# A two-layer hybrid decoder step on one core: the first layer norm split between setup and recurrence, all late modulation in the recurrence, the odd mixer's gating in the trunk

## What is computed

```python
mod = silu(c) @ ada_w[l] + ada_b[l]              # l = 0, 1; 6 * D columns
sh1, sc1, g1, sh2, sc2, g2 = split(mod, 6)
h = rms_norm(x, norm_g[l, 0]) * (1 + sc1) + sh1
m = even_mixer(h) if l == 0 else odd_mixer(h)
x = x + g1 * rms_norm(m, norm_g[l, 1])
h = rms_norm(x, norm_g[l, 2]) * (1 + sc2) + sh2
x = x + g2 * rms_norm(square(relu(h @ w1)) @ w2, norm_g[l, 3])
# inside odd_mixer
u, a, gt = split(h @ w_in)
glu = a * sigmoid(gt)
cv = depthwise_conv(concat([conv_hist, glu]), conv_w, width=31)
```

## Time and profile before

| what | us |
|---|---|
| median of 3 runs | 3334.59 |
| lowest, highest | 3334.08, 3335.05 |
| the profiled execution's own time | 3334.32 |
| span of its trace | 3332.6 |
| TensorE busy | 3019.7 (91%) |
| VectorE busy | 1193.7 (36%) |
| ScalarE busy | 971.1 (29%) |
| GpSimd busy | 540.4 (16%) |

### The profile page before, as it was taken

How to read it: one execution, slowest core, us unless ns; L and a number is a source line. 1 busy time by engine, 2 the same in 40 slices (tenths; PEclk the granted TensorE clock), 3 DMA queues, 4 the chain that set the end, 5 groups by cost and what they waited for, 6 DMA issues and landing times. The chain is left out here.

```text
span 3332.6 us, 44375 instructions
## 1 busy us (share of the span) xinstructions
PE 3019.7 (91%) x18088; PEld 2688.9 (81%) x18088; DVE 1193.7 (36%) x1924; ACT 971.1 (29%) x1418; POOL 540.4 (16%) x318
## 2 busy tenths in 40 slices
PE   5799999889877888999999998798697999999997
PEld 3689989733343788999999998793597999999997
DVE  4156552166622173222222226304345222222225
ACT  2233432257642242221111223220442211222221
POOL 1210111121112211221221211110121112211220
PEclk7899999999999889999999999899798999999998
DMA  5322222220064311211221113116221111101112
GB/s 226 114 84 83 78 83 91 91 88 1 0 185 151 117 62 50 68 59 57 69 63 56 57 57 128 44 26 145 92 87 44 32 44 50 50 29 46 50 50 96
DMA packets 240860, 250.38 MB, mean 75 GB/s; under 512 B 9203, under 2 KB 196007, under 8 KB 240453
## 3 DMA queue, kind: packets, MB, share of 16 engines
q1 hardware_dynamic: 226389, 219.53, 21.7%
q0 software_dynamic: 4320, 14.16, 1.4%
q10 hardware_dynamic: 10016, 14.80, 1.2%
HBM read 207.82 MB, written 29.99 MB: 71 GB/s over the span
## 5 line engine op out<-in xcount | busy, mean ns | idle before, releaser
L616 PE MATMUL PS<-trunk_x_hi,trunk_w_hi 128*128 128x364 f32 x2208 | 741.0, 336 | 94.9 <-POOL trunk_w_lo L763 37.5
L617 PE MATMUL PS<-trunk_x_lo,trunk_w_hi 128*128 128x364 f32 x2208 | 737.3, 334 | 0.0
L618 PE MATMUL PS<-trunk_x_hi,trunk_w_lo 128*128 128x364 f32 x2208 | 735.5, 333 | 0.0
L771 POOL TENSOR_TENSOR trunk_w_lo<-trunk_w_raw,trunk_w_hi 128x1024 fp32r<-128x1024 f32 x128 | 306.9, 2397 | 1354.6 <-ACT trunk_w_hi L979 1264.3
L616 PE MATMUL PS<-hidden,trunk_w_hi 128*128 128x364 f32 x1536 | 509.9, 332 | 0.0
L616 PEld LDWEIGHTS PS<-trunk_x_hi,trunk_w_hi 128*128 128x128 f32 x2208 | 424.2, 192 | 102.7 <-POOL trunk_w_lo L763 38.6
L617 PE MATMUL PS<-hidden,trunk_w_hi 128*128 128x364 f32 x1536 | 505.4, 329 | 0.0
L618 PE MATMUL PS<-hidden,trunk_w_lo 128*128 128x364 f32 x1536 | 505.1, 329 | 0.0
L617 PEld LDWEIGHTS PS<-trunk_x_lo,trunk_w_hi 128*128 128x128 f32 x2208 | 424.5, 192 | 0.0
L618 PEld LDWEIGHTS PS<-trunk_x_hi,trunk_w_lo 128*128 128x128 f32 x2208 | 423.7, 192 | 0.0
L1236 DVE TENSOR_TENSOR M<-M,PS 128x364 f32<-128x364 f32 x336 | 178.4, 533 | 465.2 <-PE PS L618 465.0
(11 more groups left out here) (365 smaller groups left out, 3445.4 us busy)
## 6 DMA issues: line engine op xcount, KB each, us to landing
trunk_w_raw<-mlp_w SPq DMA_DIRECT2D x128, 512.0 KB, 3.8
rec_ada_w<-ada_w SPq DMA_DIRECT2D x28, 1024.0 KB, 5.2
pages_k<-cache_sb_k SPq DMA_DIRECT2D x64, 256.0 KB, 3.0
rec_w_raw<-even_w_in SPq DMA_DIRECT2D x28, 512.0 KB, 3.8
pages_v<-cache_sb_v POOLq DMA_DIRECT2D x54, 256.0 KB, 3.4
x_scratch<-x_new ACTq DMA_DIRECT2D x9, 1456.0 KB, 5.9
trunk_ada_w<-ada_w SPq DMA_DIRECT2D x24, 512.0 KB, 3.9
x_new<-x_scratch SPq DMA_DIRECT2D x6, 1456.0 KB, 11.0
```

What stands on the lines that cost most here:

```text
L616: pe.matmul(out, hi, xh, start=first, stop=False)
L617: pe.matmul(out, hi, xl, start=False, stop=False)
L618: return pe.matmul(out, lo, xh, start=False, stop=last)
L771: pool.tensor_tensor(wl[:, u % 4, :], raw[:, u % 2, :], wh[:, u % 4, :].bitcast(F32), ALU.subtract).then_inc(s_lo, 1)
```

## The change

Six things:

1. `residual_norm` and its stage are gone. In `setup`, ScalarE squares each token tile as it lies in rows (one Square with a running sum per tile), which gives the row sums without a tree; root and reciprocal leave `core.rstd0`. ScalarE also issues the store of x's first chunk, the loads of the recurrence's first two weight tiles, and the tap rows of the odd mixer. The ring of x tiles waits for the squares as well.
2. The recurrence's program starts with nine spreading matmuls and scales, shifts and splits x in place, chunk by chunk, on VectorE and ScalarE. SyncE first stores the other two chunks. Part c of the first tile waits for chunk c of XL.
3. All 20 chunks of modulation are in the recurrence: 40 bursts, one after every second dense part, a turn after every fourth, and `coefs` takes all seven sets of coefficients. The last `mod_add` comes before the last three parts.
4. The trunk has no modulation; its loops on SyncE and ScalarE take in one more group.
5. The trunk's tail does the sigmoid (ScalarE) and the product (VectorE) of the gating.
6. The odd mixer shifts straight from `A_` (rows of 1024 columns, with zeroed margins), the first block's 16 transfers half on SyncE's and half on ScalarE's queue. Sample columns with their history go through a small tile of their own: 16 transfers on ScalarE's queue into `T4`, for which TensorE waits once, between the prompt part and the sample part of block 0. The tap columns come from setup.

The diff, cut to what the numbers speak of:

```diff
+def first_weights(nc, es, core, tag):
+    sb, sem = scope(nc, es, tag)
+    core.raw0 = sb("raw", [P, 2, KT, P])
+    core.s_raw0 = [sem(f"w_in{i}") for i in range(2)]
+def token_chunks(ap):
+    return ap.rearrange("p (k t) -> p k t", k=KT)
...
+            act.wait_ge(s_tz, 1)
+            for g in range(NTAP):
+                n = min(4, CWID - 4 * g)
+                act.dma_start(rows_tap[16 * g:16 * g + 16, 0:n * CG].rearrange("b (s c) -> b s c", c=CG),
+                              core.conv_w[0, 4 * g:4 * g + n, :].rearrange("s (b c) -> b s c", c=CG)).then_inc(s_rows, 16)
+            act.wait_ge(s_one, 1)
+            for i in range(9):
+                n = P if i < 8 else NS
+                act.wait_ge(s_xt[i % 4], 16 * (i // 4 + 1))
+                if i >= 2:
+                    act.wait_ge(s_q, i - 1)
+                act.activation(junk[0:n, i % 2, :], xt[0:n, i % 4, :], ACT.Square, accum_out=sums[0:n, i:i + 1]).then_inc(s_q, 1)
+                if i == 4:
+                    act.wait_ge(s_xev, 3)
+                    act.dma_start(token_chunks(core.x_dram)[:, :, 0:CW], X[:, :, 0:CW]).then_inc(s_st, 16)
+            w_v = core.even_w_in.rearrange("(k p) f -> p k f", p=P)
+            for i, at in enumerate((3 * HALF, 0)):
+                act.dma_start(core.raw0[:, i], w_v[:, :, at:at + P]).then_inc(core.s_raw0[i], 16)
+            act.wait_ge(s_q, 9)
+            act.wait_ge(s_rows, 16 * (11 + NTAP))
+            act.activation(sums[:, :], sums[:, :], ACT.Sqrt, scale=1.0 / D, bias=cols(core, "eps")).then_inc(s_rt, 1)
             act.wait_ge(s_c, 1)
             act.activation(core.cT[:, :, 0:SEG], PS[:, 0, 0:KT * 16].rearrange("p (k c) -> p k c", k=KT)[:, :, 0:SEG],
                            ACT.Silu).then_inc(s_silu, 1)
             ada.copies(act)
+            act.wait_ge(s_st, 16)
...
-            pe.wait_ge(s_rows, 16 * 11)
+            pe.wait_ge(s_rows, 16 * (11 + NTAP))
+            pe.transpose(PS[:, 1, 384:384 + P], rows_tap[:, :], ident)
...
+            dve.tensor_copy(core.tap_cols[:, :], PS[:, 1, 384:384 + P])
...
-def residual_norm(nc, core, tag, X, load, m, gate, scale, shift, store, final=False):
...
-            load_group(0)
-            with sp.Fori(1, G - 1) as g:
-                load_group(g, with_mod)
-            load_group(G - 1)
+            with sp.Fori(0, G) as g:
+                load_group(g)
             sp.wait_ge(s_mm, NEXT - 24)
...
-            def mod_burst(g, b):
-                pe.wait_ge(s_wa, g * 64 + 16 * (b - 3))
-                for i in range(2):
-                    k = 2 * b + i
-                    q = pe.matmul(PS[CG * (k % 4):CG * (k % 4) + SEG, 6, :], core.cT[:, k, 0:SEG], wa[:, i, :],
-                                  start=(k < 4), stop=(k >= 4), skip_group_check=True)
-                q.then_inc(s_am, 1)
...
-            with act.Fori(1, G - 1) as g:
+            with act.Fori(1, G) as g:
                 for u in range(4):
                     high_weights_of_group(g, u)
                 rest_of_group(g)
-                if with_mod:
-                    act.wait_ge(s_am, g * 4 + 1)
-                    act.activation(mod_rows[:, :], PS[:, 6, :], ACT.Copy).then_inc(s_ar, 1)
-            for u in range(4):
-                high_weights_of_group(G - 1, u)
-            rest_of_group(G - 1)
...
+                        if q == 2 and c == 0:
+                            act.wait_ge(s_nx, 12 + 8 + i + 1)
+                            act.activation(core.GT[:, i, :], core.GT[:, i, :], ACT.Sigmoid).then_inc(s_sg, 1)
...
-                    dve.wait_ge(s_at, g)
-                    dve.tensor_tensor(core.mod[:, l + 1, :].rearrange("p (f c) -> p f c", c=SEGP)[:, bass.ds(g * 4 + 4 * CH0, 4), 0:SEG],
-                                      PS[:, 7, 0:4 * SEGP].rearrange("p (f c) -> p f c", c=SEGP)[:, :, 0:SEG],
-                                      core.ada_bT[:, bass.ds(g * 4 + (48 * (l + 1) + 4 * CH0), 4)].unsqueeze(2)
-                                      .to_broadcast([P, 4, SEG]), ALU.add).then_inc(s_as, 1)
...
+            for i in range(HT):
+                dve.wait_ge(s_sg, i + 1)
+                dve.tensor_tensor(core.A_[:, i, :], core.A_[:, i, :], core.GT[:, i, :], ALU.mult)
...
-    CHUNKS = [(0, c) for c in range(4, 12)] + [(1, c) for c in range(6)]
+    CHUNKS = [(0, c) for c in range(4, 12)] + [(1, c) for c in range(12)]
...
+            for c in range(1, NC3):
+                sp.dma_start(token_chunks(core.x_dram)[:, :, c * CW:(c + 1) * CW], KV[:, :, c * CW:(c + 1) * CW])\
+                  .then_inc(s_st[c], 16)
...
-                if 0 <= n - 2 < BURSTS:
-                    modulation(n - 2)
+                for b in range(BURSTS):
+                    if max(0, (2 * b - 1) // 3) == n - 2:
+                        modulation(b)
...
+                if n == 0:
+                    pe.wait_ge(s_xl, 2 * (c + 1))
...
-                    if n % 2 == 0 and c == 0 and 2 <= n <= BURSTS:
-                        mod_turn(n // 2 - 1)
+                    d = NC3 * n + c
+                    if d % 4 == 0 and 1 <= d // 4 <= NCH:
+                        mod_turn(d // 4 - 1)
...
+            def high(c):
+                lo, hi = c * CW, c * CW + width(c)
+                for half in range(2):
+                    act.wait_ge(s_n, 2 * c + half + 1)
+                    for k in range(4 * half, 4 * half + 4):
+                        q = act.activation(core.XH[:, k, lo:hi], KV[:, k, lo:hi], ACT.Identity,
+                                           bias=core.mod[:, 0, k * SEGP:k * SEGP + 1])
+                    if half == 1 and c == NC3 - 1:
+                        act.wait_ge(s_ns, 3)
+                        q = act.activation(core.XH[:, :, SEQ:TP], KV[:, :, SEQ:TP], ACT.Copy)
+                    q.then_inc(s_xh, 1)
+            high_weights(0)
+            high(0)
+            high_weights(1)
+            high(1)
+            high(2)
             act.wait_ge(s_lb, 1)
             act.activation(lb[:, 1, :], lb[:, 0, :], ACT.Exp).then_inc(s_la, 1)
-            high_weights(0)
-            high_weights(1)
             for n in range(NT):
...
-                    if c == NC3 - 1 and n % 2 == 1 and n < BURSTS:
-                        mod_copy(n // 2)
+                    d = NC3 * n + c
+                    if d % 4 == 3 and d // 4 < NCH:
+                        mod_copy(d // 4)
...
-                for l, g, m_at, plus in ((0, 1, 2, 0.0), (0, 2, 4, 1.0), (0, 3, 5, 0.0), (1, 0, 1, 1.0)):
+                for l, g, m_at, plus in ((0, 1, 2, 0.0), (0, 2, 4, 1.0), (0, 3, 5, 0.0), (1, 0, 1, 1.0), (1, 1, 2, 0.0),
+                                         (1, 2, 4, 1.0), (1, 3, 5, 0.0)):
...
+            def normed(c):
+                lo, hi = c * CW, c * CW + width(c)
+                if c == 0:
+                    dve.wait_ge(s_bc, 1)
+                else:
+                    dve.wait_ge(s_st[c], 16)
+                if c == NC3 - 1:
+                    x = KV[:, :, SEQ:T]
+                    sh = core.mod[:, 0, :].rearrange("p (f c) -> p f c", c=SEGP)[:, 0:KT, 1:SEG]
+                    dve.tensor_tensor(x, x, norm_rows[:, SEQ:T].unsqueeze(1).to_broadcast([P, KT, NS]), ALU.mult).then_inc(s_ns, 1)
+                    dve.wait_ge(s_ns, 1)
+                    dve.tensor_tensor(segs(x), segs(x), per_seg(scale0[:, :, 1:SEG]), ALU.mult).then_inc(s_ns, 1)
+                    dve.wait_ge(s_ns, 2)
+                    dve.tensor_tensor(segs(x), segs(x), per_seg(sh), ALU.add).then_inc(s_ns, 1)
+                for k in range(KT):
+                    q = dve.scalar_tensor_tensor(out=KV[:, k, lo:hi], in0=KV[:, k, lo:hi], scalar=scale0[:, k, 0:1],
+                                                 in1=norm_rows[:, lo:hi], op0=ALU.mult, op1=ALU.mult)
+                    if k % 4 == 3:
+                        q.then_inc(s_n, 1)
...
+            def low(c, half):
+                lo, hi = c * CW, c * CW + width(c)
+                dve.wait_ge(s_xh, 2 * c + half + 1)
+                for k in range(4 * half, 4 * half + 4):
+                    q = dve.scalar_tensor_tensor(out=core.XL[:, k, lo:hi], in0=KV[:, k, lo:hi],
+                                                 scalar=core.mod[:, 0, k * SEGP:k * SEGP + 1],
+                                                 in1=core.XH[:, k, lo:hi].bitcast(F32), op0=ALU.add, op1=ALU.subtract)
...
+                q.then_inc(s_xl, 1)
+            for c in range(NC3):
+                normed(c)
+                low(c, 0)
+                low(c, 1)
             dve.memset(PS[:, 2, :], 0.0).then_inc(s_az, 1)
             dve.memset(A[:, :, :], 0.0).then_inc(s_A0, 1)
             lower_bounds()
...
-                    if n % 2 == 0 and c == 0 and 2 <= n <= BURSTS:
-                        mod_add(n // 2 - 1)
+                    d = NC3 * n + c
+                    if d % 4 == 0 and 1 <= d // 4 <= NCH:
+                        mod_add(d // 4 - 1)
...
-            mod_add(NCH - 1)
             coefs()
...
```

(78 more changed lines are left out.)

376 lines of the change are left out of this document (58 added, 318 removed).

## The result

The changed kernel takes 3292.31 us (median of 4 runs, 3289.24 to 3296.27) against 3334.82 in the same rounds: ratio 0.9874, 95% interval 0.9859 to 0.9889. Forecast were 3290.6, in a range of 3276 to 3304. The profiled execution took 3292.77, its span is 3291.1.

The account below looks back on a forecast made before the run. TensorE, at 91% of the span, was taken to bound the kernel. Start −20.7, recurrence +14.9, first trunk −33.9 and odd mixer −4 sum to −43.7, from 3334.32 to 3290.6 us; range 3276 to 3304.

Parts of the forecast that it names:

- Setup's end: Start: transfers joining setup's full load stream make it end 5 us later, ends 2 and 9.
- part goes out before the stream fills: Setup: the reason for taking 5 us instead of 6.6 for 2.54 MB of added transfers.
- Chain: Recurrence's start: spreading, scaling and splitting x by chunk, up to tile 0's third eviction, 42.9 us from its start.
- Recurrence: After tile 0's third eviction: 12 more bursts and 7 more turns, less a shorter end; +14.9 us, ends +12 and +19.
- the end's −3.5: Recurrence's end: turn, addition and coefficients come three parts earlier, so 1.9 of 5.4 us remain.
- rival C: Recurrence: modulation's weights come late, so bursts wait for their 1 MB loads; slower, 3374.6 us at 15 us per load; chance 0.03.
- ScalarE's later copies of finished chunks: Recurrence: copies wait for a burst, costed at nothing behind the heads' exponentials; without that cover, 12 us.
- Trunk: First trunk, groups 1 to 6: without modulation 576.34 instead of 610.22 us, −33.9, ends −32 and −35; gating costs nothing.
- Odd mixer: Odd mixer: shifts start at once, but convolution 0's sample part waits for T4; −4 us, ends +4 and −15.
- the prediction's signs: Odd mixer: a T4 wait of 4 to 5 us inside convolution 0 where the shifts' wait was 8.38.
- small rows fill the engines: Odd mixer: why transfers ran at only 217 GB/s on a DMA share of 0.99.
- Rival B: Start gives only 10 us if GpSimd slows each chunk and loads cost full price; 3301.3 us, chance 0.19.

Follow-up runs that it names:

- the reordering: Changed kernel with the store of x's first chunk and the first two weight tiles' loads behind the 16 modulation loads on SyncE's queue; 3290.31 us.
- clearings moved: Changed kernel with VectorE's two clearings, the lower bounds and ScalarE's exponential ahead of the recurrence's first scaling; 3284.52 us.
- the mended version: Changed kernel with five moves (clearing, spreading, loads, Silu, convolution 0's sample part), less ahead of the scaling, spreading interleaved with products; 3284.87 us, ratio 0.9843.

## Why the prediction was right, step by step

The stages moved as forecast, each within 2.1 us and for the reason given, but for the points below. That the sum came within 2 us is partly luck: the errors of the stages have both signs, and the changed kernel's own executions range from 3289.2 to 3302.6.

**Setup's end.** Forecast +5, measured +7.0. The mechanism held (full stream); the size failed at "part goes out before the stream fills". Nothing goes out free: the reordering shows 6.7 us for 2.54 MB, the 6.6 of the full price. The rate is not one number, as two windows of the changed kernel's setup show, one while the store and the weight tiles run beside the loads, one after they have landed:

```profile
25.00:40.00 15.00, 9.42 (x46) 3.56 (x48) 1.93 (x8) 4.85 (x7) 0.00 (x0) 0.63 1.08 361
45.00:50.00 5.00, 3.48 (x22) 0.89 (x15) 0.00 (x0) 0.60 (x1) 0.00 (x0) 1.00 1.05 387
```

The Trainium skill's 358 GB/s ("DMA: Bandwidth & Descriptors", Specifications) would have given 7.1. The measured 6.7 and 7.0 do not decide between 6.6 and 7.1; the 387 shows that 358 is not a ceiling for this core.

**Chain.** Forecast 42.9 us from the recurrence's start, measured 41.9. Spreading 4.37 against 4.5 (with 0.3 to begin), scaling 4.12 as in the earlier trace rows. VectorE's slowing beside GpSimd was there, but in chunk 0 (6.25 for eight low operations, 4.16 in chunk 1). So chunk 0 took 10.5 us instead of 8.4 and chunk 1 took 8.3 instead of 10.4. Both priced parts were tested: taking the spreading out gave 4.3 from the recurrence's start to the eviction, taking out what stands behind the last XL 2.2.

**Recurrence.** Forecast +14.9, measured +12.8. A burst's 1.07 and a turn's 0.80 held to the hundredth where they stand between two dense parts, the end's −3.5 too. The 2.1 between forecast and measurement are no saving of the change. TensorE's waits in front of the heads were 11.0 us in the trace of before (8.0 on line 2069 and 3.0 on line 2078) and 8.0 after; but with the odd mixer alone, where the recurrence has the instructions of before, they are 7.9. TensorE's waits there:

```profile
PE PS L2096 <- DVE M L2354: 3.0, 1, 3.0
PE PS L2087 <- issue: 2.7, 1, 2.7
PE PS L2087 <- ACT M L2225: 2.2, 2, 1.1
```

With the clearings moved, where the recurrence is as changed, they are 6.3. Each of the three waits on what is line 2069 before is 2.7 us in some executions and 1.1 in others. In the 14 traces it is 1.1 where TensorE had been granted half the clock in the 14 us before, and 2.7 where it had not, so the 3.0 go with the clock and not with the bursts' new places (last section). Counted at full clock (length times granted clock, from the traces' clock records, an estimate since waits do not scale with it) the stretch takes 509.7 us before and 523.2 after, 13.5 more; over all traces it is 508.1 to 509.7 with the old bursts and 521.1 to 523.5 with the new.

No burst waited for its load: the 40 landed in 5.0 to 11.4 us, median 5.2; rival C falls. ScalarE's later copies of finished chunks, priced at nothing, cost nothing: apart from the waits in front of the heads, TensorE has none before the stage's end.

**Trunk.** −33.94 in the six groups, as forecast. Outside them it was 1.4 longer, which is no more than executions differ by: the whole stage took 1154.5 to 1156.3 us in the three traces with modulation in the trunk and 1120.9 to 1125.2 in the eleven without. The gating at its end cost nothing, as forecast: 1122.3 us without it (modulation moved alone), 1122.0 with it.

Why the exchange pays at all was not asked: the same six chunks cost 33.9 us in the trunk and 18.4 in the recurrence. TensorE's timeline of the kernel before shows a burst of each:

```profile
127.22 1.04 PE L2050 MATMUL PS<-rec_ada_w,cT 128*9 128x512 f32 x8
...
1374.37 1.03 PE L897 MATMUL PS<-trunk_ada_w,cT 128*9 128x512 f32 x4
```

The recurrence's burst of four matmuls takes no longer than the trunk's of two, and a chunk needs two of the one or four of the other: 2.9 us with its turn against 5.0 (of the 5.6 per chunk that the trunk gave back). In either place the matmuls of a burst write to different groups of 32 partitions. What lets four pass in the time of two was not tried, and neither was a trunk with bursts of four.

**Odd mixer.** First eviction 37.5 us after the start against 37.3 forecast. The wait for T4 did not take the place of the shifts' wait, as the prediction's signs put it, but came on top: convolution 0 begins 8.0 us earlier, though still behind 7.18 us of waiting, and loses 3.42 (forecast 4 to 5) to T4. In the eight traces that have this odd mixer with convolution 0's sample part in this place, the first eviction comes 37.1 to 37.9 us after the start, in the three with the old one 41.3 to 43.3, so the 4 us are clear here, where the whole time does not show them. That T4 was the only thing between the two convolutions is shown by taking it away. The words "small rows fill the engines" are not shown: the shifts' rows of before are 5.3 KB long, setup's loads read rows of 2 KB, and these moved 386 GB/s. Why 217 GB/s fill the engines stays open.

**Rival B** (the start gives half) falls with 19.7.

## What to carry to other kernels

Price a transfer that joins a full stream at its whole size, and put it behind what the next stage waits for, if its own user comes later: that one reordering would have added a third to the start's gain. Work hidden under a wait loses its cover when another edit takes the wait away; so price two moves together before adding them. Before moving work between two stages, compare what one piece of it costs in each; here the gain came from that difference. And before putting a smaller wait down to a change, look for the same wait in a kernel without it.

## What was not expected

Executions of one kernel differ by more than the three runs shown beforehand let one think: the kernel before took from 3329.7 to 3343.2 us in later rounds. The traces show one place where they differ. The rest of the recurrence in three executions with the same instructions there (clearings moved; as changed; all shifts on SyncE), windows view:

```profile
97.34:629.72 532.38, 523.95 (x3496) 472.11 (x3494) 210.49 (x318) 174.59 (x236) 62.75 (x26) 0.98 0.35 108
228.60:232.10 3.50, 3.50 (x14) 1.19 (x12) 0.00 (x0) 0.93 (x2) 0.00 (x0) 0.51 0.00 0
```

```profile
100.23:645.14 544.91, 535.00 (x3496) 476.50 (x3494) 210.43 (x318) 174.68 (x236) 62.69 (x26) 0.96 0.34 105
223.00:231.00 8.00, 8.00 (x60) 7.31 (x59) 0.00 (x0) 1.42 (x2) 2.35 (x1) 1.00 0.01 2
231.00:238.00 7.00, 7.00 (x23) 3.84 (x22) 0.00 (x0) 2.74 (x4) 0.00 (x0) 0.51 0.32 85
```

Between them stands 538.54 at 0.97 for the kernel as changed. With two digits of clock, length times granted clock is good to some 2.7 us; the traces' clock records give 0.981, 0.971 and 0.959, and 522.1, 523.2 and 522.7 us. So the work is the same, and nearly all of the 12.5 us hangs on how long TensorE was granted 1.2 instead of 2.4 GHz: 20.5, 30.7 and 44.4 us, of which half is lost. The second and third row of the last fence are one such dip: full clock in the first 8 us, then half for 7. Before it fell, TensorE ran 16 instructions of 8 columns (line 1876, eight matmuls) and the first matmul of 512 columns behind them; in the execution with the short time, the dip at the same place lasted 3.5 us (second row of the first fence). What decides between 3.5 and 7 was not tried. Other stages differ too: the shortest profiled execution of all (3280.07, the mended version) has 544.8 us in this stretch. For a change of 4 us in such a kernel, an event's place in its own stage tells more than the whole time, as the odd mixer alone shows.
